# Seven pieces of the modulation products moved into the two norms with shifts, and the order of products and values in sparse attention

## The reference, cut

```python
def first_block(x, c, ...):                       # 256 tokens x 1024
    c_act = jax.nn.silu(c)
    for i in range(2):
        mod = c_act @ ada_w[i] + ada_b[i]         # 1024 -> 6 * 1024
        sh1, sc1, gt1, sh2, sc2, gt2 = jnp.split(mod, 6, axis=-1)
        h = _rmsnorm(x, norm_g[i, 0]) * (1 + sc1) + sh1
        y = short_conv(h) if i == 0 else rwkv7(h)
        x = x + gt1 * y
        h = _rmsnorm(x, norm_g[i, 1]) * (1 + sc2) + sh2
        x = x + gt2 * (jnp.square(jax.nn.relu(h @ mlp_w1[i])) @ mlp_w2[i])
    return _rmsnorm(x, final_g)

def second_block(x, ...):
    h = x + dsa_attention(rms_norm(x, ...), ...)  # sparse: 16 heads, top 64 keys of a row
    h = h + sq_relu_mlp(...)
    h = h + fox_attention(...)
    h = h + sq_relu_mlp(...)
    return rms_norm(h, g_final)
```

## Time and profile before

| | |
|---|---|
| median of 3 runs | 1488.87 us (1488.63 to 1492.4) |
| the profiled execution | 1487.04 us |
| its span, first to last instruction | 1485.2 us |
| PE matmul busy | 1408.3 us (95%) |
| DVE / ACT / POOL busy | 887.2 / 698.4 / 115.5 us |
| mean granted TensorE clock | 0.977 |
| HBM traffic | 172 GB/s over the span |

### The profile page before, as it was taken

One profiled execution on the slowest core, in us unless ns is written; L12 is line 12 of the kernel. 1 busy time (PEld: TensorE's weight loads), 2 busy tenths in 40 slices (PEclk: granted clock), 3 DMA queues, 4 the chain that ended last, 5 costly groups with the idle time before them and its releaser, 6 DMA issues.

```text
span 1485.2 us, 27037 instructions
## 1 busy us (share of the span) xinstructions
PE 1408.3 (95%) x11631; PEld 1200.0 (81%) x11631; DVE 887.2 (60%) x1368; ACT 698.4 (47%) x1192; POOL 115.5 (8%) x114
## 2 busy tenths in 40 slices
PE   4999999999899899988999998899999999999997
PEld 1897778879698899767888887678888899888886
DVE  1447634446647645557556668766665668676555
ACT  2434533334367323445444544655444557564443
POOL 0000000010100544320000001000000012000000
PEclk8999999999999999989999999999999999999999
DMA  9998799945234200014665542236656454365661
GB/s 359 382 332 298 254 360 303 308 156 170 89 114 142 87 4 4 3 39 164 199 197 178 179 142 86 98 100 200 192 176 199 146 170 139 118 213 176 194 197 57
DMA packets 177423, 257.07 MB, mean 173 GB/s; under 512 B 10424, under 2 KB 122360, under 8 KB 177304
## 3 DMA queue, kind: packets, MB, share of 16 engines
q1 hardware_dynamic: 177304, 255.35, 52.2%
HBM read 254.28 MB, written 1.05 MB: 172 GB/s over the span
## 4 chain that ended last, share of the span: by engine, by line
PE 87%; DVE 5%; ACT 3%; issue 1%; DMA 1%; SPq 1%; POOL 0%; DVEq 0%; ACTq 0%; POOLq 0%
PE acc L2023 10%; PE acc L2024 9%; PE acc L2025 9%; PE un L1968 8%; PE un L1970 7%; PE un L1969 7%; PE side L2006 6%; PE un L2006 6%; PE acc L2290 4%; PE side L2007 3%; PE un L2007 3%; PE side L2133 3%; PE side L2290 2%; DMA ada_buf<-in_ada_w 1%; DVE w_lo L1322 1%
## 5 line engine op out<-in xcount | busy, mean ns | idle before, releaser
L1322 DVE TENSOR_TENSOR w_lo<-stage,w_hi 128x1024 fp32r<-128x1024 f32 (+1 forms) x378 | 457.4, 1247 | 271.3 <-ACT w_hi L783 270.6
L783 ACT ACTIVATE w_hi<-stage 128x1024 fp32r<-128x1024 f32 (+1 forms) x378 | 380.3, 1050 | 249.2 <-PE acc L2025 215.7
L2023 PE MATMUL acc<-w_hi,z_hi 128*128 128x512 f32 x640 | 253.5, 396 | 0.7 <-DVE pair_logit L1806 0.7
L2024 PE MATMUL acc<-w_lo,z_hi 128*128 128x512 f32 x640 | 250.2, 391 | 0.0
L2025 PE MATMUL acc<-w_hi,z_lo 128*128 128x512 f32 x640 | 249.9, 390 | 0.0
L1968 PE MATMUL un<-h_both,w_hi 128*128 128x256 f32 x768 | 227.1, 296 | 3.0 <-DVE h_both L1380 2.8
L1969 PE MATMUL un<-h_both,w_hi 128*128 128x256 f32 x768 | 218.9, 285 | 0.0
L1970 PE MATMUL un<-h_both,w_lo 128*128 128x256 f32 x768 | 218.8, 285 | 0.0
L1968 PEld LDWEIGHTS un<-h_both,w_hi 128*128 128x128 f32 x768 | 149.0, 194 | 18.4 <-issue 10.1
L1969 PEld LDWEIGHTS un<-h_both,w_hi 128*128 128x128 f32 x768 | 149.1, 194 | 1.3 <-issue 1.2
L1970 PEld LDWEIGHTS un<-h_both,w_lo 128*128 128x128 f32 x768 | 148.9, 194 | 0.0
(11 more groups left out here) (365 smaller groups left out, 1984.8 us busy)
## 6 DMA issues: line engine op xcount, KB each, us to landing
stage<-in_mlp_w SPq DMA_DIRECT2D x64, 1024.0 KB
ada_buf<-in_ada_w SPq DMA_DIRECT2D x48, 1024.0 KB, 7.7
stage<-in_w_up SPq DMA_DIRECT2D x32, 1024.0 KB
stage<-in_w_down SPq DMA_DIRECT2D x32, 1024.0 KB
stage<-in_conv_w_in SPq DMA_DIRECT2D x12, 1024.0 KB
stage<-in_rw_w_rkv SPq DMA_DIRECT2D x12, 1024.0 KB
stage<-in_w_in_a SPq DMA_DIRECT2D x8, 1024.0 KB
stage<-in_w_kv_b SPq DMA_DIRECT2D x8, 1024.0 KB
```

What stands on the lines that cost most here:

```text
L783: A_(w_hi[u % 2][:, half, 0:n], stage[u % NSTAGE][:, half, 0:n], ACT.Copy).then_inc(hi_made, 1)
L1322: V.tensor_tensor(w_lo[u % 2][:, half, 0:n], stage[u % NSTAGE][:, half, 0:n], w_hi[u % 2][:, half, 0:n].bitcast(F32), ALU.subtract).then_i ...
L2023: MM(y, z_hi[:, kt, q], wh[:, i, :], start=(first and kt == 0), stop=False, skip_group_check=True)
L2024: MM(y, z_hi[:, kt, q], wl[:, i, :], start=False, stop=False, skip_group_check=True)
```

## The change

Slots 0 to 13 keep their piece. Slot 14 takes two (22 and 23), slot 15 none, slots 16 to 32 one each (27 to 43), the slots behind none. Pieces 24 and 25 stand in place of `keep_warm` ahead of the norm of the first MLP, 26 behind its `turn_first`; pieces 44 to 47 stand in place of `keep_warm` ahead of the RWKV layer's norm. Set 5 is turned in slot 15, set 11 (now in the bank `un[0]`, products and turns) after four tiles of the RWKV layer; PE waits for its addition before the second unit of that layer. The places of copies, turns and additions of a set are now tables. `xs_rw`, a ring buffer and `ada_row` move to other addresses, so that they don't meet. POOL waits for 44 pieces. In sparse attention the products of pair 1 follow those of pair 0, and the products of pair p + 1 stand directly ahead of the values of pair p - 1.

```diff
-        xs_sq, xs_rw = at("xs_sq", [P, QT, D], sq_off), at("xs_rw", [P, QT, D], r_off[2])
+        xs_sq = at("xs_sq", [P, QT, D], sq_off)
+        xs_rw = at("xs_rw", [P, QT, 2, D], act_off[2])[:, :, 0, :]
...
-        ada_off = act_off + [tmp_off] + r_off[0:5]
+        ada_off = act_off + [tmp_off] + r_off[0:4] + [r_off[4] + 1024]
...
+        ADA_MLP_IN, ADA_RW_IN = (24, 25, 26), (44, 45, 46, 47)
         def ada_after(slot):
-            return ADA_FIRST + slot if ADA_FIRST + slot < N_ADA else None
+            if slot == 14:
+                return (22, 23)
+            if slot == 15:
+                return ()
+            if slot < 14:
+                return (8 + slot,)
+            return (11 + slot,) if slot <= 32 else ()
+        TURNED_AT = {4: 2, 8: 3, 12: 4, 15: 5, 18: 6, 22: 7, 26: 8, 30: 9, 34: 10}
...
         def ada_sums(s):
-            return un[0] if s == 1 else misc
+            return un[0] if s in (1, LAST_SET) else misc
...
-            pool.wait_ge(ada_used, N_ADA)
+            pool.wait_ge(ada_used, ADA_RW_IN[0])
...
                 split(u + 4)
+                if n == N_MLP0:
+                    copy_set(COPIED_AT[S_OUT + 2])
...
                 mix_split(m)
+                if m == 1:
+                    copy_set(LAST_SET)
...
+            add_set(LAST_SET)
             mod_gain(1, 1)
...
             last_units(U_CONV_OUT, z_ready(Z_CONV))
-            keep_warm(V_MLP[0], 3)
+            for k in ADA_MLP_IN[:2]:
+                ada_products(k)
             turn_first(N_MLP0)
+            ada_products(ADA_MLP_IN[2])
             mlp(0, N_MLP0)
             pe.wait_ge(row_out, 2)
-            keep_warm(V_RKV, 3)
+            free_bank(V_RKV + 1)
+            for k in ADA_RW_IN:
+                ada_products(k)
             turn_first(N_RW)
...
+                if t == 3:
+                    turn_set(LAST_SET)
...
+                if j == 1:
+                    pe.wait_ge(ada_added, ADA_SETS)
...
             for p in range(PAIRS):
                 if p:
-                    a_products(p)
                     pair_turns(0, p - 1)
+                else:
+                    a_products(1)
...
+                if 0 < p < PAIRS - 1:
+                    a_products(p + 1)
                 if p:
                     a_values(p - 1)
```

More of the change, by code:

```diff
@@ L184, in build @@
         vec_in = at("vec_in", [P, 3, P], scr_off + 8192)
-        ada_off = act_off + [tmp_off] + r_off[0:5]
+        ada_off = act_off + [tmp_off] + r_off[0:4] + [r_off[4] + 1024]
         ada_buf = [at(f"ada_buf{i}", [P, 2, D], o) for i, o in enumerate(ada_off)]
-        ada_row = [at(f"ada_row{i}", [P, 2 * P], r_off[5] + 1024 * i) for i in range(2)]
+        ada_row = [at(f"ada_row{i}", [P, 2 * P], r_off[5] + 4096 + 1024 * i) for i in range(2)]
         c_silu = small[:, 0:8]
@@ L486, in ada_src, with ada_turns @@
             return w[2 * P * q:2 * P * (q + 1), D * (s % 6):D * (s % 6 + 1)].rearrange("(t p) n -> p t n", p=P)
+        ADA_MLP_IN, ADA_RW_IN = (24, 25, 26), (44, 45, 46, 47)
         def ada_after(slot):
-            return ADA_FIRST + slot if ADA_FIRST + slot < N_ADA else None
[L492 to L502, removed]
+            if slot == 14:
[5 more added lines that the diff above has]
+            return (11 + slot,) if slot <= 32 else ()
+        COPIED_AT = {3: 2, 7: 3, 11: 4, 14: 5, 16: 6, 20: 7, 24: 8, 28: 9, 32: 10}
+        TURNED_AT = {4: 2, 8: 3, 12: 4, 15: 5, 18: 6, 22: 7, 26: 8, 30: 9, 34: 10}
+        ADDED_AT = {5: 2, 9: 3, 13: 4, 17: 5, 19: 6, 23: 7, 27: 8, 31: 9, 35: 10}
+        LAST_SET = ADA_SETS - 1
         S_CONV, S_OUT, S_MLP = 0, 12, 16
         def ada_sums(s):
-            return un[0] if s == 1 else misc
-        ada_turns = stat_ps
+            return un[0] if s in (1, LAST_SET) else misc
+        def ada_turns(s):
+            return un[0][:, 0, :] if s == LAST_SET else stat_ps[:, s % 2, :]
         WKV_LEVELS = range(1, 6)
@@ L951, in mlp @@
                             split_half(uu + 2, 1)
[L952 to L955, removed]
+                            if m == 0 and g == GROUPS - 1:
+                                row_copy(1, stat_ps, misc)
+                        if m == 0:
+                            copy_set(COPIED_AT.get(S_MLP + 2 * UPD * g + j))
                         if g == 0 and m >= 2:
@@ L1604, in _ @@
                     z_split(Z_CONV + k, k)
[L1605 removed]
+                add_set(ADDED_AT.get(S_CONV + j))
             def last_gain():
                 for j in range(UPD):
[L1608 removed]
+                    add_set(ADDED_AT.get(S_OUT + j))
                 mod_gain(0, 1)
@@ L2142, in turn_set @@
                 for b in range(2):
-                    ins = nc.tensor.transpose(ada_turns[:, s % 2, P * b:P * b + P], ada_row[s % 2][:, P * b:P * b + P], ident)
+                    ins = nc.tensor.transpose(ada_turns(s)[:, P * b:P * b + P], ada_row[s % 2][:, P * b:P * b + P], ident)
                 ins.then_inc(ada_turned, 1)
             def ada_piece(slot):
-                if ada_after(slot) is not None:
-                    ada_products(ada_after(slot))
-                if ada_set_turned_at(slot) is not None:
-                    turn_set(ada_set_turned_at(slot))
+                for k in ada_after(slot):
+                    ada_products(k)
+                if slot in TURNED_AT:
+                    turn_set(TURNED_AT[slot])
             def mlp(m, n):
```

18 lines of the change are left out of this document (8 added, 10 removed).

## The result

The changed kernel takes 1480.43 us in the median of 4 runs (1480.04 to 1482.3), the kernel before in the same comparison 1488.75 us (1488.23 to 1492.4). In two later comparisons the same two kernels gave 0.9937 (0.9912 to 0.9962) and 0.9929 (0.9904 to 0.9953). The forecast was 1480.1.

A forecast was written before the change was run, and what follows sets the result against it. TensorE (PE) was taken as the bound, 87% of the span. Pieces 6.54, turns of a set 0.19, clock at the second place 1.65 and sparse attention 0.43 sum to 8.81 us: 1488.87 to 1480.1 us, range 1477 to 1484.

The forecast's parts named there:

- the distance between the norms: Sign: the gap between the two norms with shifts shrinks; less than 7 us would prove the prediction wrong.
- the attention: Sign: sparse attention moves by no more than 1 us; more would prove the prediction wrong.
- the clock at the second place: RWKV layer's norm: clock stays 1.00 for the first low-rank products, which take 2.8 us; 1.65 us saved, bounds 0 to 1.65.
- the start of the first unit: Sign at the first MLP's norm: the first normalised unit starts 1.0 to 1.1 us later than 159.15.
- A piece between two units: Convolution and first MLP: each piece between units costs 1.09 us of PE; 39 paid before, 33 after.
- The extra piece in slot 14: Before the first MLP's norm: a second piece in slot 14 moves all that follows by 1.09 us.
- the 6.54 of the sum: Saving from pieces between units: 6 x 1.09 = 6.54 us.
- Cover at the first place: First MLP's norm: set 5's turn and pieces 24 to 26 fit PE's waits, at nothing; no clock loss, bound 1.65 us.
- rival 2: Clock falls at the first place, its fillers gone: gain 7.16, 1481.7 us; if the second falls too, 5.5, 1483.4; chance 0.16.
- The transfers: Pieces' transfers on SyncE's queue: all in time, cost nothing; closest is piece 32, by 1.6 us.
- rival 4: Ring of pieces comes late: with 15 us landings, 17 pieces from slot 16 hold PE 17 us, 1497.1 us; chance 0.04.
- Sparse attention, 0.43: Sparse attention: ACT's exponentials of the second pair start 0.43 us earlier, later waits follow; bounds 3.5 gained, 0.9 lost.

## Why the prediction was right, point by point

- **The number.** 1480.1 forecast, 1480.43 measured. It was right through terms that were off in both directions, and that the two agree to 0.3 us is luck: the interval of the ratio is 6 us wide, and the traces of the first pair add up to 7.0 us gained, not 8.8. Of the signs named, the distance between the norms shrank by more than 7 us (8.85) and the attention moved by less than 1; the clock at the second place and the start of the first unit (1.6 us later, not 1.0 to 1.1) were not as said in the first profile.
- **A piece between two units, 1.09 us each: too small.** It is 1.20. The step that failed read the distance to the first product of the next unit and didn't look at the second. For the seven pieces behind the first place this is 0.8 us more gained; the count (39 paid before, 33 after) held.
- **The extra piece in slot 14: 0.86 us, not 1.09.** It stands in a row with another. From the last product of the unit before to the first of the next it was 1.32 us with one piece (144.82 to 146.14) and is 2.18 with two:

```profile
144.57 0.39 PE L2035 MATMUL acc<-w_hi,z_lo 128*128 128x512 f32 x1
144.89 1.93 PE L2143 MATMUL side<-ada_buf,c_rep 128*32 128x256 f32 x32
146.75 0.50 PE L2033 MATMUL acc<-w_hi,z_hi 128*128 128x512 f32 x1
```

  By these prices the pieces gave 7 x 1.20 - 0.86 = 7.54 us, 1.0 more than the 6.54 of the sum. That the first row of the table, +0.95, lies near its forecast of 1.09 is chance: the turn of set 5 adds 0.22 to it (from the last product of the unit to the first piece it is 0.54 us now, and was 0.32), and the convolution's length differs by 0.5 to 1.0 us between executions of the same code anyway.
- **Cover at the first place, taken at nothing: failed.** The pieces fitted into PE's waits as worked out, piece 26 too (with the clock kept, PE still waits 0.37 us for the first normalised tile). But the clock fell, which I had priced as rival 2 at 0.16: six executions of six, 1.05 to 1.15 us in the five that can be compared and not the bound of 1.65, since PE would have waited in a part of the slow stretch anyway (0.37 us ahead of the unit, with the clock kept). The step that failed is "3.6 us, about as today, then piece 26: no loss taken". The stretch did stay as long as it was (3.75 us against 3.8). What changed in it is the wait: two of 0.99 and 1.37 us before, one of 2.52 now. My own numbers had it (through at 155.3, half a microsecond of transposes, the next group at 158.1, which is a wait of 2.3), and I compared only the whole stretches. That filling the wait keeps the clock is shown by four executions; that its length is what decides is the reading of the table and not shown.
- **The clock at the second place, 1.65: right in four executions of six.** Price and cause were right, as the kernel before with twice the fillers shows. Four pieces in a row take 3.66 us and not 4.4: 0.92 for each, so the part of the price that lies at the two ends of a piece is paid once for the row. So they end earlier than forecast, and the wait behind them is 1.74 us where the forecast's numbers leave about 1. My argument for the term compared stretches (3.5 us after the change, as at the first place); the stretch is 4.3.
- **The transfers: no wait of PE for a piece behind the start.** The margin was thin, as forecast. SP's queue, then piece 33's landing and its use:

```profile
190.16 1.37 SPq L585 DMA_DIRECT2D ada_buf<-in_ada_w  x1
...
193.60 0.91 SPq L585 DMA_DIRECT2D ada_buf<-in_ada_w  x1
...
DMA to landing us min/median/max: 11.8/11.8/11.8
...
208.56 1.07 PE L2143 MATMUL side<-ada_buf,c_rep 128*32 128x256 f32 x16
```

  It is needed 15.0 us behind its issue and landed after 11.8; piece 32, the one that I named, had 11.7 us and took 8.7. The 20.7 us that rival 4 was built on the earlier trace rows is a landing at the start; behind 40 us the longest in that trace was 13.3. Rival 4 did not come near.
- **Sparse attention, 0.43:** 0.4 to 0.6, by the mechanism named.
- **The Trainium skill's rule** in "TensorE: Matmul & The Clock Gate", Part 4, that transposes don't count as busy in the same way for the clock gate: the transposes at 154.50 in the changed kernel did not hold the clock, as the rule has it. But by the rule alone, with the pieces counted as full work, the first place before and after the change is alike, 3.8 and 3.75 us without counted work, and the clock was kept four times of four in the one and lost six of six in the other. No run here separates the transposes of the one from the wait of the other.

What stays open: whether it is the longest wait or something that goes with it which decides at the two places (the table orders them, no run changed the wait alone, and narrow pieces may count for less than full-width work); why the second place keeps the clock in some executions and not in others, with the same instructions and waits; and whether falls saved at the two places come back in the recurrence.

## What to carry to other kernels

Price an insertion by the distance between two instructions that are far enough on either side to be undisturbed, and price a row of insertions apart from a single one. Work that replaces a filler has the filler's second duty, to hold the clock until dense work resumes: compare PE's waits behind each, and top the work up with a filler where the longest has grown. And compare two traces stretch by stretch before calling a forecast right: here the pieces were worth 1.0 us more than forecast and the first place 0.8 to 0.9 us less, and the total shows neither.

## What the runs showed of the hardware

- Products with a stationary operand of 32 columns hold the granted clock: 7.9 us of nothing but such pieces, transposes and waits kept it in four executions of six, where 5.4 us of transposes and waits lost it in four of four; with pieces last at the first place it stayed 1.00 in one execution (157 to 160.5). Whether they hold it as well as full-width products is open.
- Two stretches of 3.8 and 3.75 us at the same place, one with waits of 0.99 and 1.37 us, the other with one of 2.52 and narrow pieces around it, kept the clock in four executions of four and lost it in six of six; a third, 4.3 us with waits of 1.74 and 1.00, lost it in two of six, with the same instructions each time.
- Executions differ by what the clock loses, in steps of some 1.7 us: 17.1 to 23.9 us lost in a stretch of 540 us, whose length went from 538.7 to 545.1 us with it. For a single kernel, the changed one, it was 17.1 to 22.2 us and 538.7 to 544.0.
- A row of 32-column products costs less for each piece than one alone: 1.20 us for one between two units, 0.86 for the second of two, 0.92 for each of four.
